# Peer experts' first matrix: both halves of x as one operand of 512 columns, whole banks stored, summed and passed through gelu in the second stage

## The reference, cut to what matters

```
q = (xb @ w_query).reshape(tokens, 8, 2, 128)
s = einsum('thpc,pkc->thpk', q, sub_keys)          # scores, top 16 of each half, top 16 of the sums
e, g = expert numbers, softmax of their scores
act = gelu(einsum('td,thkd->thk', xb, expert_u[e]))
y   = einsum('thk,thkd->td', g * act, expert_v[e])
```

## Time and profile before

| | |
|---|---|
| median of 3 runs | 1290.45 us (1290.4 to 1290.52) |
| profiled execution | 1290.7 us, its span 1288.9 us |
| instructions | 21561 |
| busy: PE, DVE, ACT, POOL | 99%, 74%, 53%, 3% of the span |
| first expert stage | from 536 to 934.6 us of the span |
| second expert stage | from 934.6 to 1282.8 us |

### The profile page before, as it was taken

How to read it: one execution, slowest core, us unless ns; L and a number is a source line. 1 busy time by engine, 2 the same in 40 slices (tenths; PEclk the granted TensorE clock), 3 DMA queues, 4 the chain that set the end, 5 groups by cost and what they waited for, 6 DMA issues and landing times.

```text
span 1288.9 us, 21561 instructions
## 1 busy us (share of the span) xinstructions
PE 1279.4 (99%) x8375; PEld 1156.8 (90%) x8375; DVE 952.9 (74%) x1733; ACT 689.5 (53%) x1161; POOL 34.7 (3%) x29
## 2 busy tenths in 40 slices
PE   9999999999999999999999999999999999999998
PEld 8899988888878889999999999999988888888886
DVE  6776568884467767999999777777776676766676
ACT  6666467553455754444454555555555444555545
POOL 0000030000020010000000000000000000000000
PEclk9999999999999999999999999999999999999999
DMA  8543456656656445577767656566677767776763
GB/s 267 164 135 128 132 179 198 195 181 198 193 165 222 131 144 174 148 243 232 235 218 229 217 184 208 185 193 198 196 271 272 243 243 245 244 241 240 242 242 114
DMA packets 72805, 260.53 MB, mean 202 GB/s; under 512 B 8256, under 2 KB 9024, under 8 KB 72448
## 3 DMA queue, kind: packets, MB, share of 16 engines
q1 hardware_dynamic: 71232, 255.25, 61.1%
q0 software_dynamic: 1040, 3.34, 0.8%
q10 hardware_dynamic: 432, 0.56, 0.1%
HBM read 240.25 MB, written 18.87 MB: 201 GB/s over the span
## 4 chain that ended last, share of the span: by engine, by line
PE 95%; DVE 2%; ACT 1%; POOL 1%; issue 0%; DVEq 0%; ACTq 0%
PE ps L1096 27%; PE ps L483 16%; PE ps L491 12%; PE ps L492 12%; PE ps L493 12%; PE ps L502 4%; PE ps L1057 2%; PE ps L505 2%; PE ps L549 1%; PE ps L536 1%; PE ps L680 1%; POOL wlo L2419 1%; PE ps L542 1%; PE ps L530 1%; PE ps L1016 1%; PE ps L513 0%
## 5 line engine op out<-in xcount | busy, mean ns | idle before, releaser
L1644 DVE TENSOR_TENSOR wlo<-raw,whi 128x1024 fp32r<-128x1024 f32 (+2 forms) x410 | 497.6, 1215 | 262.8 <-ACT whi L1133 258.5
L1133 ACT ACTIVATE whi<-raw 128x1024 fp32r<-128x1024 f32 (+2 forms) x421 | 441.9, 1050 | 396.5 <-PE ps L1096 168.9
L491 PE MATMUL ps<-T,whi 128*128 128x256 f32 x1264 | 363.9, 288 | 0.0
L492 PE MATMUL ps<-T,whi 128*128 128x256 f32 x1264 | 357.2, 283 | 0.0
L493 PE MATMUL ps<-T,wlo 128*128 128x256 f32 x1264 | 357.2, 283 | 0.0
L1096 PE MATMUL ps<-whi,T 128*128 128x512 f32 x1024 | 315.5, 389 | 0.0
L492 PEld LDWEIGHTS ps<-T,whi 128*128 128x128 f32 x1264 | 242.1, 192 | 0.0
L491 PEld LDWEIGHTS ps<-T,whi 128*128 128x128 f32 x1264 | 242.0, 191 | 0.0
L493 PEld LDWEIGHTS ps<-T,wlo 128*128 128x128 f32 x1264 | 241.9, 191 | 0.0
L1096 PEld LDWEIGHTS ps<-whi,T 128*128 128x128 f32 x1024 | 192.2, 188 | 39.9 <-DVE wlo L1644 0.2
L1096 PE MATMUL ps<-wlo,T 128*128 128x512 f32 x512 | 199.2, 389 | 0.0
(11 more groups left out here) (326 smaller groups left out, 1403.6 us busy)
## 6 DMA issues: line engine op xcount, KB each, us to landing
raw<-in_expert_u_dram SPq DMA_DIRECT2D x128, 512.0 KB, 3.7
raw<-in_expert_v_dram SPq DMA_DIRECT2D x128, 512.0 KB, 3.8
raw<-in_w_up_dram SPq DMA_DIRECT2D x32, 512.0 KB, 4.2
raw<-in_w_down_dram SPq DMA_DIRECT2D x32, 512.0 KB, 4.2
acts<-stage SPq DMA_DIRECT2D x32, 512.0 KB, 4.2
stage<-acts SPq DMA_DIRECT2D x30, 512.0 KB, 3.3
raw<-in_w_in_dram SPq DMA_DIRECT2D x20, 512.0 KB, 4.2
raw<-in_w_gate_dram SPq DMA_DIRECT2D x16, 512.0 KB, 3.5
```

Of the source, the lines that this page charges most:

```text
L491: e.matmul(dst, whi[:, h, sl], xh[:, k, :], start=k == 0, stop=False)
L492: e.matmul(dst, whi[:, h, sl], xl[:, k, :], start=False, stop=False)
L1133: e.activation(whi[:, u % NH, 0:n], raw[:, u % NR, 0:n], ACT.Copy).then_inc(*hi(u))
L1644: e.tensor_tensor(wlo[:, u % NH, 0:n], raw[:, u % NR, 0:n], whi[:, u % NH, 0:n].bitcast(F32), ALU.subtract).then_inc(*lo(u))
```

## The change

The first stage's product of `whi` with both halves of x becomes one matmul of 512 columns over a whole bank, through `wide_cols`; the products of `wlo` are added to its first half. ACT no longer applies gelu there: it copies the whole bank (512 columns) into one of four slots of `stage`, and SP stores each unit by itself (256 KB). Only four units (124 to 127) stay in `stage`. In the second stage DVE adds the two halves of a slot (`total`), ACT applies gelu to the sum in place (`gelu_v`), and DVE takes it (`take`); SP fetches each unit by itself.

```diff
-V_ORDER = [*range(120, 128), *range(120)]
+V_ORDER = [*range(124, 128), *range(124)]
-        acts = nc.dram_tensor("acts", (32, 128, 4, 256), F32).ap()
+        acts = nc.dram_tensor("acts", (124, 128, 512), F32).ap()
-        stage = sb(p4, "stage", [128, 8, 256])
+        stage = sb(p4, "stage", [128, 4, 512])
-        gb4, squares, fin = ACTV[:, 120:124, :]...
+        gb4, squares, fin = ACTV[:, 124:128, :]...
-        d_store = [landing(f"store{i}", range(i, 32, 2)) for i in range(2)]
-        d_fetch = [landing(f"fetch{i}", range(i, 30, 2)) for i in range(2)]
+        d_store = [landing(f"store{i}", range(i, 124, 4)) for i in range(4)]
+        d_fetch = [landing(f"fetch{i}", range(i, 124, 4)) for i in range(4)]
# PE, first stage
             for n in range(128):
-                whole(EU + n)
...
-                    e.wait_ge(*gelu_u.at(n - 4))
-                m = cols(EU + n, 0, 8, TH, TL, ps[b][:, 0:256], range(4))
...
-                cols(EU + n, 0, 8, TH, TL, ps[b][:, 0:256], range(4, 8)).then_inc(*used(EU + n))
+                    e.wait_ge(*kept_u.at(n - 4))
+                if n in (HOT_FROM + 1, 127):
+                    m = wide_cols(EU + n, T, 4 + n % 4, range(4))
+                    if n == 127:
+                        m.then_inc(*half_used("u"))
+                    else:
+                        for g in hot_groups(HOT_FROM):
+                            weigh(g)
+                    wide_cols(EU + n, T, 4 + n % 4, range(4, 8)).then_inc(*used(EU + n))
+                else:
+                    wide_cols(EU + n, T, 4 + n % 4, range(8)).then_inc(*used(EU + n))
# ACT
             def take_u(n):
                 e.wait_ge(*used.at(EU + n))
-                if n >= 8:
-                    e.wait_ge(*d_store[n // 4 % 2].at(n // 4 - 2))
-                e.activation(stage[:, n % 8, :], ps[4 + n % 4][:, 0:256], ACT.Gelu_apprx_tanh).then_inc(*gelu_u(n))
+                if n >= 4:
+                    e.wait_ge(*d_store[n % 4].at(n - 4))
+                copy(stage[:, n % 4, :], ps[4 + n % 4][:, :]).then_inc(*kept_u(n))
+
+            def gelu_v(i):
+                h = stage[:, V_ORDER[i] % 4, 0:256]
+                e.wait_ge(*summed.at(i))
+                e.activation(h, h, ACT.Gelu_apprx_tanh).then_inc(*gelu_h(i))
...
+                if n == 120:
+                    warm(ACT.Gelu_apprx_tanh)
                 if n == 127:
+                    gelu_v(1)
                     split(EV + 1)
-                    for i in range(3):
-                        cut(i)
+                    cut(0)
+                    cut(1)
                 else:
                     split(EU + n + 2)
                 if n:
                     take_u(n - 1)
+                if n == 126:
+                    gelu_v(0)
+                if n == 127:
+                    gelu_v(2)
+                    cut(2)
...
+            gelu_v(3)
             for n in range(125):
-                if n + 2 > 2:
+                if n:
                     cut(n + 2)
+                if n < 124:
+                    gelu_v(n + 4)
                 split(EV + n + 2)
# DVE
+            def total(i):
+                v = V_ORDER[i]
+                if i < 4:
+                    e.wait_ge(*kept_u.at(v))
+                else:
+                    e.wait_ge(*d_fetch[v % 4].at(v))
+                at = stage[:, v % 4, :]
+                e.tensor_tensor(at[:, 0:256], at[:, 0:256], at[:, 256:512], ALU.add).then_inc(*summed(i))
             def take(i):
                 v = V_ORDER[i]
-                if i < 8:
-                    e.wait_ge(*gelu_u.at(v))
-                elif i % 4 == 0:
-                    e.wait_ge(*d_fetch[v // 4 % 2].at(v // 4))
+                e.wait_ge(*gelu_h.at(i))
...
                 if n == 127:
-                    for i in range(3):
-                        take(i)
+                    total(1)
+                    take(0)
+                    take(1)
                     cut(0)
                     split(EV + 1)
                     cut(1)
-                    take(3)
+                    total(2)
+                    take(2)
                     cut(2)
                 else:
                     split(EU + n + 2)
+                if n == 126:
+                    total(0)
...
+            total(3)
             for n in range(125):
+                take(n + 3)
+                if n < 124:
+                    total(n + 4)
                 if n:
-                    take(n + 3)
                     cut(n + 2)
                 split(EV + n + 2)
# SP
-            def store(j):
-                e.wait_ge(*gelu_u.at(4 * j + 3))
-                e.dma_start(acts[j], stage[:, 4 * (j % 2):4 * (j % 2) + 4, :]).then_inc(*d_store[j % 2](j))
+            def store(v):
+                e.wait_ge(*kept_u.at(v))
+                e.dma_start(acts[v], stage[:, v % 4, :]).then_inc(*d_store[v % 4](v))
+            def fetch(v):
+                if v < 4:
+                    e.wait_ge(*d_store[v].at(120 + v))
+                e.wait_ge(*taken_v.at(v))
+                e.dma_start(stage[:, v % 4, :], acts[v]).then_inc(*d_fetch[v % 4](v))
...
             for n in range(128):
                 load(EU + n + 5)
-                if n % 4 == 0 and n:
-                    store(n // 4 - 1)
+                if 0 < n < 125:
+                    store(n - 1)
+            fetch(0)
+            fetch(1)
             load(EV + 5)
-            store(31)
+            fetch(2)
             load(EV + 6)
-            fetch(0)
             for n in range(2, 125):
-                if n % 4 == 0 and n < 120:
-                    fetch(n // 4)
+                if n < 123:
+                    fetch(n + 1)
                 load(EV + n + 5)
```

More of the change, by code:

```diff
@@ L258, in twice @@
             return bc(ps[b][:, 0:256].rearrange("p (g t) -> p g t", t=4), 3, 2)
-        gb4, squares, fin = ACTV[:, 120:124, :].rearrange("p a b -> p (a b)"), raw[:, 1, :], raw[:, 2:4, :]
+        gb4, squares, fin = ACTV[:, 124:128, :].rearrange("p a b -> p (a b)"), raw[:, 1, :], raw[:, 2:4, :]
         r1, ss1, v1, s1 = stat(2), stat(2), stat(2), stat(2)
@@ L401, in build @@
         score_a = signal("score_a", range(4))
-        gelu_u = signal("gelu_u", range(128))
+        kept_u = signal("kept_u", range(128))
+        gelu_h = signal("gelu_h", range(128))
         weight_a = signal("weight_a", range(64))
@@ L458, in build @@
         hot = signal("hot", range(64))
+        summed = signal("summed", range(128))
         taken_v = signal("taken_v", range(128))
@@ L1063, in tensor_program @@
                     score(3)
-                whole(EU + n)
-                b = 4 + n % 4
                 if n in (0, 1):
@@ L2328, in one_hots @@
                                 ALU.mult).then_inc(*hot(g))
+            def total(i):
[6 more added lines that the diff above has]
+                e.tensor_tensor(at[:, 0:256], at[:, 0:256], at[:, 256:512], ALU.add).then_inc(*summed(i))
             def take(i):
                 v = V_ORDER[i]
-                if i < 8:
-                    e.wait_ge(*gelu_u.at(v))
-                elif i % 4 == 0:
-                    e.wait_ge(*d_fetch[v // 4 % 2].at(v // 4))
+                e.wait_ge(*gelu_h.at(i))
                 if i == 0:
                     e.wait_ge(*weight_a.at(63))
-                e.tensor_tensor(ACTV[:, v, :], ACTV[:, v, :], stage[:, v % 8, :], ALU.mult).then_inc(*taken_v(i))
+                e.tensor_tensor(ACTV[:, v, :], ACTV[:, v, :], stage[:, v % 4, 0:256], ALU.mult).then_inc(*taken_v(i))
             def cut(i):
```

## The result

The changed kernel takes 1360.62 us (median of 4 runs, 1360.06 to 1361.05), beside 1290.49 for the kernel before on the same chip: a ratio of 1.0543, 95% interval 1.0525 to 1.0561. The forecast was 1360.5.

A forecast was written before the change was run, and what follows sets the result against it. PE (busy 1279.4 of 1288.9 us) bounds the kernel before; a ring of waits bounds the second stage after. 1290.7 - 10.9 + 2.6 + 77.8 + 0.6 = 1360.8, median 0.25 lower: 1360.5 us; range 1347 to 1381.

The forecast's parts named there:

- Part 1: First-stage matmuls: the wider mix runs at 2.794 us a unit against 2.880, saving 10.9 us up to unit 127.
- The 0.013 us for each matmul saved: PE: two 256-column matmuls cost 0.013 us more than one of 512, from the paces of the two expert stages.
- Part 2: First stage's ACT copy, DVE work and transfers: hidden behind PE, costing nothing; DMA share 0.90.
- Part 3, the ring: Second stage: total, gelu, ACT's split, DVE's split, take, next total wait in a closed loop, 3.35 us a unit.
- First and last units: EV begins 2.96 us after unit 127, EV+2 about 11.0 after it, 2.6 us late; the end adds 0.6.
- The sum: Whole kernel: 10.9 us saved, 2.6, 77.8 (123 turns) and 0.6 added to 1290.7 give 1360.8; median 1360.5.
- (a): Second stage: by busy shares total and gelu fit in idle time, PE stays the bound, 1281 us; chance 0.06.
- (b): Second stage: fetches land late, total waits; decides above 6.7 us, 1 us a turn costs 123 us; chance 0.04.
- (c): Second stage: PE's pauses lower its clock; at the slowest pace the stage costs 290 us more; chance 0.02.
- (d): First stage doesn't gain, held by DVE or the DMA share: up to 11 us more, 1371; chance 0.10.
- the prediction's own signs of being wrong: Second stage keeps 2.718 us, DVE's addition waits for the fetch, or the granted clock falls.
- PE's idle ahead of its second-stage matmuls: Second stage: PE idles some 75 us in all there, released by DVE's split.

The follow-up runs named there:

- experiment 2: Changed kernel with the first stage's matmuls narrow again, 1 of 512 and 22 of 256 columns a unit: 1369.70 us.
- Experiments 3 and 4: The pair: experiment 3, and the changed kernel with the same unused DVE addition between take(n+3) and total(n+4) instead, 1401.63 us.
- experiment 1: Changed kernel with ACT's split(EV+n+2) put ahead of gelu(n+4) in each second-stage turn: 1283.42 us, ratio 0.9954 to the kernel before.
- experiment 6: Changed kernel with each second-stage fetch on SP one place earlier, ahead of the load it stood behind: 1359.25 us.
- experiment 3: Changed kernel with one more unused 128x256 DVE addition a second-stage turn, between cut(n+2) and split(EV+n+2): 1361.37 us.

## Why the prediction was right, step by step

**Part 1, 10.9 us: right, measured 10.3.** The pace of `w_up` carried over (2.793). What is missing is the second half of the stage: from unit 66 on, where the gates' matmuls stand between, a unit took 3.380 us before and 3.307 now, by the starts of ACT's splits; that is 0.073 saved and not 0.087. The 0.013 us for each matmul saved, worked out beside the sum from two stages' paces, was a little high: it would give 0.107 a unit, and the runs show 0.087/8 = 0.011 (experiment 2: 0.080/7 = 0.011). The Trainium skill (TensorE: Matmul & The Clock Gate, "Back-to-back issue gap") gives 2.5 ns beyond the columns for an isolated matmul; carried over to this stream it would have made the saving 2.6 us, and the runs show four times that.

**Part 2, the rest of the first stage at nothing: right.** PE is filled there; DVE reached 47.22 of 50 us and the DMA share 0.86 (forecast 0.90).

**Part 3, the ring at 3.35 us: right, measured 3.33.** Each term came out within 0.01: 0.42 + 0.03 + 0.32 + 1.08 + 1.14 + 0.34. The measured turn lies on the lower bound of 3.33, though gelu at its own lower bound of 0.32 gives 3.34. The exp of the routing was a good stand-in for a gelu that the trace of before never showed from SBUF. Experiments 3 and 4 show that it is the ring and not DVE's load; experiment 1 that the ring is closed by one place in ACT's order.

**First and last units: right.** EV began 3.11 us behind unit 127 for 2.96, EV+2 11.08 us behind it for 11.0; the end cost 0.2 us for 0.6.

**The sum, 77.8 us for 123 turns: 77.6 measured, by two small errors that cancel.** The ring is 3.333 us (60 turns from 1141.72 to 1341.71 by the starts of gelu), so 123 x 0.017 = 2.1 us less, and one late fetch makes it 1.9 us more (experiment 6). The mechanism was right, but that the whole forecast came within 0.2 us is partly luck: part 1 gave 0.6 us less than forecast, the second stage and the end cost 0.6 less.

**The rivals.** (a), the reading by busy shares, would have been right for another order of the same instructions: experiment 1 lies at 1283.4 where it had 1281. The averages were true; they say what could fit, not what does. (b), transfers: it named a landing above 6.7 us as the point from which it decides, and the one fetch that took 7.98 us cost a wait in its turn, as that says; the median of 4.2 us is not the 3.3 that I took from fetches twice as large:

```profile
stage<-acts SPq DMA_DIRECT2D x124, 256.0 KB, 4.2
```

(c), the clock, fell twice for a few us without a cost (last section). (d) came about in small only, as the 0.6 us of part 1. Of the prediction's own signs of being wrong two showed for a moment, a wait of DVE's addition for a fetch and a lower granted clock. The signs were too sharp: each would have needed an amount.

**What was forecast and did not show.** PE's idle ahead of its second-stage matmuls was put at 75 us; PE's row has 41.7. Of the 0.61 us that a turn is longer, the row shows 0.32: the last matmul's recorded 0.39 us reaches 0.16 beyond its pace into the pause, and the first of the next unit holds up the second by 0.11 (0.34 for 0.227). The starts give the 0.61.

## What to carry to other kernels

Where two in-order engines hand work to each other more than once in a turn, write down each engine's instructions in order and follow the waits until they close; where the sum around that ring is more than the fullest engine needs (here 3.33 us against PE's 2.72), it is the turn, however idle the engines look. In this kernel an instruction inside the ring cost its full time in every turn (41.0 us), and one in a wait that was longer than it cost almost nothing (0.75 us): so a new hand-over goes behind the instruction that the next stage waits for. When such a ring has been opened, look at the transfers again, since the shorter turn gives them less time.

## What the runs showed of the hardware

PE's clock. The pause of 0.6 us in every turn left the granted clock at 1.00 nearly throughout. But in the changed kernel it fell twice to its lower level (1.2 GHz) for a few us: behind PE's pause of 2.26 us where the stages meet, and behind the one of 2.33 us at the late fetch. Windows of it (columns as in the earlier trace rows, the granted clock third from the end):

```profile
932.00:936.00 4.00, 3.54 (x11) 2.83 (x12) 2.90 (x7) 1.67 (x3) 0.53 (x1) 0.73 0.62 181
936.00:940.00 4.00, 4.00 (x16) 3.21 (x16) 2.90 (x7) 1.90 (x4) 0.00 (x0) 0.84 0.98 305
996.00:1000.00 4.00, 2.22 (x7) 1.79 (x8) 2.40 (x5) 2.34 (x5) 0.00 (x0) 0.84 0.29 92
```

In the timeline of PE above, the pace goes from about 0.23 us a matmul to 0.42 (934.47 to 934.89) there. It cost nothing: PE has 0.6 us to spare in each turn and was level with the ring again after a few units, and DVE's splits stayed 3.33 us apart there. The profile of experiment 3 has the same two pauses (2.26 and 2.29 us) and a granted clock of 1.00 behind both; so the pause alone does not settle it, and no run here shows what does.

A fetch of 256 KB lands in 4.2 us, one of 512 KB took 3.3 before: it now leaves right behind a load of 512 KB in every turn, and before it left ahead of one in every fourth. Half the bytes are not half the time to landing. Whether the place in the queue is the cause is not shown: no run moves it alone.
